# Router products of a two-layer expert stage: three bfloat16 matmuls per token from one comparison, in four PSUM banks

## What is computed

```python
def chunk(xc):
    q = (xc @ w_query).reshape(c, PEER_HEADS, 2, PEER_HALF_DIM)
    sc = jnp.einsum('chpd,hpnd->chpn', q, keys32)
    sv, si = lax.top_k(sc, PEER_TOPK)
    cand = (sv[:, :, 0, :, None] + sv[:, :, 1, None, :]).reshape(c, PEER_HEADS, -1)
    cidx = (si[:, :, 0, :, None] * PEER_N_KEYS + si[:, :, 1, None, :]).reshape(c, PEER_HEADS, -1)
    best, pos = lax.top_k(cand, PEER_TOPK)
    eidx = jnp.take_along_axis(cidx, pos, axis=-1)
    g = jax.nn.softmax(best, axis=-1)
    a = jnp.einsum('cd,chkd->chk', xc, w_up[eidx])
    act = jax.nn.gelu(a, approximate=False) * g
    return jnp.einsum('chk,chkd->cd', act, w_down[eidx])
```

## Time and profile before

| | us |
|---|---|
| median of 3 runs | 2591.95 (2590.22 to 2592.58) |
| profiled execution | 2590.26, span 2588.4 |
| TensorE busy | 2452.9 |
| VectorE busy | 1677.3 |
| ScalarE busy | 1345.7 |

### The profile page before, as it was taken

How to read it: one execution, slowest core, us unless ns; L and a number is a source line. 1 busy time by engine, 2 the same in 40 slices (tenths; PEclk the granted TensorE clock), 3 DMA queues, 4 the chain that set the end, 5 groups by cost and what they waited for, 6 DMA issues and landing times.

```text
span 2588.4 us, 44433 instructions
## 1 busy us (share of the span) xinstructions
PE 2452.9 (95%) x15412; PEld 2201.5 (85%) x15412; DVE 1677.3 (65%) x2990; ACT 1345.7 (52%) x2514; POOL 35.5 (1%) x82
## 2 busy tenths in 40 slices
PE   8989999999999998999999999999999899988988
PEld 7889999999888887989998999888888787776866
DVE  4646998777655555656998677655565537546454
ACT  4545555777555444444445777545555425534533
POOL 1000000000000000000000000000000000000000
PEclk9999999999999999999999999999999869789999
DMA  6344555444566664655555444566655523134443
GB/s 216 113 141 153 172 177 163 131 124 125 174 191 194 193 194 149 185 171 156 170 179 155 131 129 125 171 194 192 213 179 181 167 66 91 58 107 146 146 123 114
DMA packets 136853, 398.45 MB, mean 154 GB/s; under 512 B 12336, under 2 KB 13568, under 8 KB 135696
## 3 DMA queue, kind: packets, MB, share of 16 engines
q1 hardware_dynamic: 134144, 384.97, 48.3%
q0 software_dynamic: 2576, 11.71, 1.5%
HBM read 395.59 MB, written 1.05 MB: 153 GB/s over the span
## 4 chain that ended last, share of the span: by engine, by line
PE 69%; DVE 21%; ACT 5%; issue 5%; POOL 0%; DMA 0%; DVEq 0%; ACTq 0%; POOLq 0%; SPq 0%
PE bank L893 27%; PE bank L877 11%; PE bank L776 11%; PE bank L782 7%; DVE wl L1446 7%; PE bank L905 3%; ACT first L1255 2%; PE bank L843 2%; PE bank L831 2%; ACT wh L1142 1%; DVE arena L1613 1%; DVE arena L1614 1%; DVE arena L1616 1%; DVE arena L1615 1%; PE bank L974 1%
## 5 line engine op out<-in xcount | busy, mean ns | idle before, releaser
L1446 DVE TENSOR_TENSOR wl<-raw,wh 128x1024 fp32r<-128x1024 f32 (+1 forms) x732 | 893.4, 1222 | 635.0 <-ACT wh L1142 623.7
L1142 ACT ACTIVATE wh<-raw 128x1024 fp32r<-128x1024 f32 (+1 forms) x732 | 771.5, 1055 | 669.9 <-PE bank L893 341.7
L877 PE MATMUL bank<-xh,wh 128*128 128x256 f32 x2048 | 513.4, 288 | 5.3 <-issue 3.4
L877 PE MATMUL bank<-xl,wh 128*128 128x256 f32 x2048 | 502.5, 283 | 0.0
L877 PEld LDWEIGHTS bank<-xh,wh 128*128 128x128 f32 x2048 | 392.6, 192 | 7.4 <-DVE pairs L1684 3.8
L877 PEld LDWEIGHTS bank<-xl,wh 128*128 128x128 f32 x2048 | 393.2, 192 | 0.0
L877 PE MATMUL bank<-xh,wl 128*128 128x256 f32 x2048 | 293.0, 286 | 6.8 <-DVE wl L1446 6.8
L893 PE MATMUL bank<-wh,gl 128*128 128x512 f32 x1024 | 274.2, 390 | 1.7 <-DVE gl L1723 1.7
L893 PE MATMUL bank<-wh,gh 128*128 128x512 f32 x1024 | 274.0, 389 | 0.5 <-ACT gh L1272 0.5
L877 PEld LDWEIGHTS bank<-xh,wl 128*128 128x128 f32 x2048 | 262.9, 191 | 13.0 <-DVE wl L1446 11.5
L893 PE MATMUL bank<-wl,gh 128*128 128x512 f32 x1024 | 273.7, 389 | 0.0
(11 more groups left out here) (247 smaller groups left out, 2800.4 us busy)
## 6 DMA issues: line engine op xcount, KB each, us to landing
raw<-in_w_upT SPq DMA_DIRECT2D x256, 512.0 KB, 3.5
raw<-in_w_down SPq DMA_DIRECT2D x256, 512.0 KB, 3.5
raw<-in_l_w_in SPq DMA_DIRECT2D x84, 512.0 KB, 3.7
raw<-in_peer_w_query SPq DMA_DIRECT2D x32, 512.0 KB, 3.9
raw<-in_l_w_out SPq DMA_DIRECT2D x28, 512.0 KB, 3.7
raw<-in_attn_w_qkv SPq DMA_DIRECT2D x24, 512.0 KB, 4.3
raw<-in_conv_w_in SPq DMA_DIRECT2D x24, 512.0 KB, 3.8
arena<-in_na_bias POOLq DMA_DIRECT2D x4, 1024.0 KB, 6.0
```

The lines of the kernel that those rows point to most:

```text
L877: last = pe.matmul(banks[b][:, 0:SEQ], lhsT=w[part][:, k, :], rhs=x_in[xp][:, k, :], start=(k == 0 and part == 0 and xp == 0), stop=(k == ...
L1142: act.activation(wh[:, n % SPLIT, 0:kts * cols], raw[:, n % RAW, 0:kts * cols], ACT.Copy)\
L1446: tt(wl[:, n % SPLIT, 0:kts * cols], raw[:, n % RAW, 0:kts * cols], wh[:, n % SPLIT, 0:kts * cols].bitcast(F32), ALU.subtract).then_inc(lo ...
```

## The change

RING stays four; two more constants are FIRSTS = 3 (buffers of weighted first keys) and OUTS = 4 (banks for products, 2 to 5). Both one-hot rows come from one bf16 comparison against `key_pairs`. The weight is split in three bf16 parts ahead of the stage; ScalarE multiplies the first one-hot with the first part as before, VectorE with the two others. TensorE accumulates three bf16 matmuls per token with the same stationary one-hot. `idxT` takes its banks from the ring of banks 4 to 7, TensorE no longer waits for its reads, and the low parts of tiles 70 and 71 move behind the copies of each token tile. VectorE no longer waits for first_weighted; it waits for its own comparison ahead of the multiplications, and TensorE and both multiplying engines wait for the semaphores shown.

```diff
--- before.py
+++ after.py
@@ -84,7 +84,7 @@
 HALF = N_KEYS // 2
 QUAD = 4
 QUADS = SEQ // QUAD
-RING = 4
+RING, FIRSTS, OUTS = 4, 3, 4
 FIRST, SLOTS = 72, 54
 WIDE, NARROW = 4, 4
 CANDS = WIDE * TOPK + (TOPK - WIDE) * NARROW
@@ -281,16 +281,16 @@
         at = place_of["aux"]
         lanes = place("lanes", [P, N_KEYS], BF16, at)
         at += 2 * N_KEYS
-        choice = place("choice", [P, 3, SEQ], F32, at)
-        at += 4 * 3 * SEQ
-        pairs = place("pairs", [P, SEQ, 2], BF16, at)
-        at += 2 * 2 * SEQ
-        second = place("second", [P, RING, QUAD, N_KEYS], F32, at)
-        at += 4 * RING * QUAD * N_KEYS
-        chosen = place("chosen", [P, 2, QUAD, N_KEYS], BF16, at)
-        at += 2 * 2 * QUAD * N_KEYS
-        first = place("first", [P, RING, QUAD, N_KEYS], F32, at)
-        at += 4 * RING * QUAD * N_KEYS
+        weight_high = place("weight_high", [P, SEQ], F32, at)
+        at += 4 * SEQ
+        key_pairs = place("key_pairs", [P, SEQ, 2, 2], BF16, at)
+        at += 2 * 4 * SEQ
+        rest_pairs = place("rest_pairs", [P, 2, SEQ, 2], BF16, at)
+        at += 2 * 4 * SEQ
+        onehot = place("onehot", [P, RING, QUAD, 2, N_KEYS], BF16, at)
+        at += 2 * RING * QUAD * 2 * N_KEYS
+        first = place("first", [P, FIRSTS, 3, QUAD, N_KEYS], BF16, at)
+        at += 2 * FIRSTS * 3 * QUAD * N_KEYS
         late = place("late", [P, 2, SEQ], F32, at)
         at += 4 * 2 * SEQ
         gh, gl = (place(n, [P, SPLIT, SEQ], F32R, at + k * 4 * SPLIT * SEQ) for k, n in enumerate(("gh", "gl")))
@@ -369,9 +369,9 @@
                 J.add("wo", 4, own=False, ring="projection")
             J.add("na", len(na_steps(n)), ring="other")
             J.add("na_oT", NA_JOINED.count(n), ring="other")
-        J.add("norm_peer0", 4); J.add("query0", 8, own=False); J.add("scores0", 8); J.add("idxT0", 2)
+        J.add("norm_peer0", 4); J.add("query0", 8, own=False); J.add("scores0", 8); J.add("idxT0", 2, ring="other")
         J.add("norm_conv", 4); J.add("conv_in", 12, own=False); J.add("conv_out", 4, own=False)
-        J.add("norm_peer1", 4); J.add("query1", 8, own=False); J.add("scores1", 8); J.add("idxT1", 2)
+        J.add("norm_peer1", 4); J.add("query1", 8, own=False); J.add("scores1", 8); J.add("idxT1", 2, ring="other")
         J.add("norm_mem", 4, ring="projection"); J.add("mem0", 2, own=False, ring="projection"); J.add("mem1", 2, own=False, ring="projection")
         EV, OM = attention_order(sum(n for _, n in SEC)), attention_order(MEM_HEADS)
 
@@ -443,6 +443,7 @@
         top_ready, top_exp = sem("top_ready"), sem("top_exp")
         top_split = sem("choices_split")
         onehots, first_weighted = sem("onehots_ready"), sem("first_keys_weighted")
+        rests_weighted = sem("first_keys_weighted_by_rests")
         products, weighted = sem("router_products"), sem("experts_weighted")
         held, late_weighted = sem("router_weights_held"), sem("late_experts_weighted")
         gelu_done = sem("gelu_done")
@@ -897,14 +898,15 @@
 
                 def router(q):
 
-                    pe.wait_ge(onehots, q0 + q + 1)
                     pe.wait_ge(first_weighted, q0 + q + 1)
-                    if q >= 2:
-                        pe.wait_ge(weighted, q0 + q - 1)
+                    pe.wait_ge(rests_weighted, q0 + q + 1)
+                    if q >= OUTS:
+                        pe.wait_ge(weighted, q0 + q - OUTS + 1)
                     for c in range(QUAD):
-                        last = pe.matmul(banks[2 + q % 2][:, c * N_KEYS:(c + 1) * N_KEYS],
-                                         lhsT=second[:, q % RING, c, :], rhs=first[:, q % RING, c, :],
-                                         start=True, stop=True)
+                        for p in range(3):
+                            last = pe.matmul(banks[2 + q % OUTS][:, c * N_KEYS:(c + 1) * N_KEYS],
+                                             lhsT=onehot[:, q % RING, c, 1, :], rhs=first[:, q % FIRSTS, p, c, :],
+                                             start=(p == 0), stop=(p == 2))
                     last.then_inc(products, 1)
 
 
@@ -923,8 +925,6 @@
                     for i in range(3):
                         last = pe.transpose(bank(j)[:, i * P:(i + 1) * P], top_out(t, i), ident[:])
                     done(last, j)
-                for t in range(TT):
-                    wait_read(pe, J.of(f"idxT{layer}", t))
                 for t in range(FIRST - 2, FIRST):
                     up(t)
 
@@ -1248,12 +1248,12 @@
                 def weigh_first(q):
 
                     act.wait_ge(onehots, q0 + q + 1)
-                    if q >= RING:
-                        act.wait_ge(products, q0 + q - RING + 1)
+                    if q >= FIRSTS:
+                        act.wait_ge(products, q0 + q - FIRSTS + 1)
                     for c in range(QUAD):
                         c0 = q * QUAD + c
-                        ins = act.activation(first[:, q % RING, c, :], chosen[:, q % 2, c, :], ACT.Copy,
-                                             scale=choice[:, 2, c0:c0 + 1])
+                        ins = act.activation(first[:, q % FIRSTS, 0, c, :], onehot[:, q % RING, c, 0, :], ACT.Copy,
+                                             scale=weight_high[:, c0:c0 + 1])
                     ins.then_inc(first_weighted, 1)
 
                 def hold(q):
@@ -1261,7 +1261,7 @@
                     n = tiles_before(q)
                     act.wait_ge(products, q0 + q + 1)
                     act.activation(acts[:, n:N_KEYS, q * QUAD:(q + 1) * QUAD],
-                                   banks[2 + q % 2].rearrange("p (c i) -> p i c", c=QUAD)[:, n:N_KEYS, :], ACT.Copy)\
+                                   banks[2 + q % OUTS].rearrange("p (c i) -> p i c", c=QUAD)[:, n:N_KEYS, :], ACT.Copy)\
                         .then_inc(held, 1)
 
                 def gated_high(t, i=0):
@@ -1605,7 +1605,10 @@
                 part_f = scratch(5, HK)
                 pick = view(P_KEYS, PEER_HEADS, TOPK, TOPK)
                 red = scratch(PEER_HEADS)
-                assert off[0] <= ARENA
+                choice = scratch(3, P)
+                rest_of = scratch(P)
+                assert off[0] + P // 2 <= ARENA
+                rounded = place(f"rounded{layer}", [P, P], BF16, place_of["arena"] + 4 * off[0])
 
                 def top16(values, index, src, tmp):
 
@@ -1680,8 +1683,16 @@
                     j = J.of(f"idxT{layer}", t)
                     wait_filled(dve, j)
                     cols = slice(t * P, (t + 1) * P)
-                    step(dve.tensor_copy(choice[:, :, cols], bank(j)[:, 0:3 * P].rearrange("p (a b) -> p a b", a=3)))
-                    read_out(dve.tensor_copy(pairs[:, cols, :], choice[:, 0, cols].unsqueeze(2).to_broadcast([P, P, 2])), j)
+                    step(dve.tensor_copy(choice, bank(j)[:, 0:3 * P].rearrange("p (a b) -> p a b", a=3)))
+                    step(dve.tensor_copy(rounded[:], choice[:, 2]))
+                    read_out(dve.tensor_copy(key_pairs[:, cols].rearrange("p c a b -> p a c b"),
+                                             choice[:, 0:2].unsqueeze(3).to_broadcast([P, 2, P, 2])), j)
+                    dve.tensor_copy(weight_high[:, cols], rounded[:])
+                    step(tt(rest_of, choice[:, 2], rounded[:], ALU.subtract))
+                    step(dve.tensor_copy(rest_pairs[:, 0, cols], rest_of.unsqueeze(2).to_broadcast([P, P, 2])))
+                    step(tt(rest_of, rest_of, rest_pairs[:, 0, cols, 0], ALU.subtract))
+                    dve.tensor_copy(rest_pairs[:, 1, cols], rest_of.unsqueeze(2).to_broadcast([P, P, 2]))
+                    low(u0 + FIRST - 2 + t)
                 dve.wait_ge(extra_loaded["lanes"], 16 * (layer + 1))
                 q0 = QUADS * layer
 
@@ -1690,15 +1701,19 @@
                     s = q % RING
                     if q >= RING:
                         dve.wait_ge(products, q0 + q - RING + 1)
-                    if q >= 2:
-                        dve.wait_ge(first_weighted, q0 + q - 1)
-                    c0 = q * QUAD
-                    lane = lanes[:].rearrange("p (n b) -> p n b", b=2).unsqueeze(1).to_broadcast([P, QUAD, N_KEYS // 2, 2])
-                    key = pairs[:, c0:c0 + QUAD, :].unsqueeze(2).to_broadcast([P, QUAD, N_KEYS // 2, 2])
-                    tt(chosen[:, q % 2].rearrange("p c (n b) -> p c n b", b=2), lane, key, ALU.is_equal)
-                    last = tt(second[:, s], lanes[:].unsqueeze(1).to_broadcast([P, QUAD, N_KEYS]),
-                              choice[:, 1, c0:c0 + QUAD].unsqueeze(2).to_broadcast([P, QUAD, N_KEYS]), ALU.is_equal)
-                    last.then_inc(onehots, 1)
+                    c0, w = q * QUAD, N_KEYS // 2
+                    hot = onehot[:, s].rearrange("p c a (n b) -> p (c a) n b", b=2)
+                    lane = lanes[:].rearrange("p (n b) -> p n b", b=2).unsqueeze(1).to_broadcast([P, 2 * QUAD, w, 2])
```

(17 more changed lines are left out.)

## The result

The median of six runs is 2547.87 us (2537.03 to 2551.42), against 2591.13 us (2589.76 to 2592.58) for the kernel before: a ratio of 0.9826 with a 95% interval of 0.9804 to 0.9847, 43.3 us less. The profiled execution took 2551.42 us (span 2549.5), 38.9 us less in the span. Of eleven further runs of the kernel before, taken beside r1 to r4, one took 3329.7 us at a mean granted clock of 0.669 and counts in no comparison; the median of the other ten is 2591.56 us.

The account below looks back on a forecast made before the run. TensorE was taken to set the pace, VectorE having some 60 us to spare. Per layer -9.3 - 11.3 + 1.9 + 1.0 = -17.7 us, two layers -35.4, gave 2556.5 us, range 2548 to 2584.

Parts of the forecast that it names:

- The waits for banks: Late expert tiles: four product banks remove 8.9 us of TensorE waits and 2.4 of cold starts, 11.3 us per layer.
- The cover that I named for ScalarE in double places: Where two quads fall between the same two tiles: 0.85 us before ScalarE's lateness makes TensorE wait; failing is an 8% rival.
- The router's matmuls: Router, 64 quads per layer: twelve bf16 pairs at 0.062 us take 0.744 us instead of 0.89, gaining 9.3 us per layer.
- The slow pairs: Rival at the router: a bf16 pair takes 0.111 us like an fp32 record, +19 us per layer, 2630 us; 8%.
- the half-hidden load: Rival at the router: half the weight load shows, 0.080 us a pair, only -4.9 us per layer, 2582 us; 9%.
- VectorE at its limit: Late expert tiles: VectorE, at 1.40 us per quad, just keeps up; TensorE's waits for low parts cost 1.0 us per layer.
- the cost of the last tile, 3.74 us: End of the stage: VectorE's work per tile, with its quads, set against TensorE's 3.76 us, so nothing to spare.
- my own ends: VectorE's work per tile with its quads: 3.31 us early in the stage, 3.74 us at its end.
- the rival with quicker pairs: Router: pairs of 0.055 us, VectorE holding the last third, bring 4 us more per layer, about 2549 us; 10%.
- Ahead of the stage: From the transposes to the first tiles: VectorE's longer work before each low part costs 1.9 us per layer, 1 to 3.
- the clock at 1.5 us either way: Behind the transposes in layer 1: whether the clock falls to 1.2 GHz again was left open, 1.5 us either way.

Follow-up runs that it names:

- r1: The changed kernel run again with nothing altered: 2543.07 us median, ratio 0.9825 to the kernel before.
- r4: The changed kernel with only VectorE's order ahead of the stage altered, low parts of weight tiles before the copies: 2537.27 us median, ratio 0.9798 to the kernel before.
- r2: The kernel before with four product banks instead of two and nothing else: 2561.16 us median, ratio 0.9882.
- r5: The changed kernel without the third matmul per token, executed once: 194.2 us from router(0) to the first down tile, against 204.6.
- r3: The changed kernel with two product banks instead of four: 2571.11 us median, ratio 0.9918 to the kernel before.
- r7: The changed kernel with three product banks instead of four, executed once: 204.6 us from router(0) to the first down tile, as with four.

## Why the prediction was right in its direction and short in its size

Of the 43.3 us, the two stages and their passages carry 20.2 + 21.5 = 41.7 us in the profile (238.0 to 217.8 us, and 239.4 to 217.9 us, from the transposes to down). The forecast had 35.4. The difference of 6.3 us has three terms; the rest of the program gives 1.6 us in the medians, and the median of before itself came out 0.8 us lower with more runs (2591.13 for 2591.95). That makes up the 8.6 us.

*The waits for banks: right.* 11.3 us per layer, by r2 to the tenth. This is more than half of what the change brings, and needs none of its bf16 work. The cover that I named for ScalarE in double places held: no wait for scalings or a high part in the stage.

*The router's matmuls: mechanism right, term too small. This is the largest error.* I took 0.062 us a pair from small fp32 pairs; it takes 0.056 us, within 3 ns of 128 cycles of 2.4 GHz. What I put at nothing is the way from the tile to the pairs and back, 0.07 us in each of 54 places. Per layer 54 quads became 0.16 us cheaper and ten 0.23 us, which gives the measured 10.9 us (r2 to the changed kernel) where I had 9.3. That is 3.2 us of the error in both layers. The two mistakes work against each other: the cheaper pairs bring 64 x (0.23 - 0.146) = 5.4 us more per layer than I had, and the places take back 54 x 0.07 = 3.8. So that 9.3 came as near as it did is in part luck. My own 0.057 us (cycles plus the 4 ns of the same line) was the better price of a pair, but it would have given 13.2 us, further off. The slow pairs (0.111 us) and the half-hidden load (0.080 us) are excluded: the loads of 128 bf16 columns add at most 3 ns to the spacing. With them falls the sentence of the Trainium skill (TensorE: Matmul & The Clock Gate, "Back-to-back issue gap") on a stream of pairs at about 81 ns: here it is 56 ns, near what the same page's isolated gap gives.

*VectorE at its limit: wrong.* I charged 1.0 us per layer, 2.0 in all; measured is none. The durations were right (1.40 us per build, to the hundredth). The step that failed compared the cost of the last tile, 3.74 us, with TensorE's 3.76 and made waits of it. That the last tiles have nothing to spare was right (VectorE is busy for 99% of the time from 620 to 640 us), but TensorE did not wait. Up to there VectorE needs less than TensorE and gets ahead, so the sum over the stage counts: the mean of my own ends, 3.53 us over 54 places, is 190 us, and r5 measured a floor of 194.2 at most against 204.6. The same step held up the low end of the range: I let VectorE stop the rival with quicker pairs at 2549 us. By its sum it would have stopped nothing before 194 us per stretch, and without it that rival comes to about 2544 us (5.4 us per layer off the forecast, and the 1.0 us gone).

*Ahead of the stage: right in layer 0, too dear in layer 1.* I said 1.9 us per layer; it is 2.0 and 0.7. The steps came as listed, and the low parts behind the copies are what costs, as r4 shows. In layer 1 the kernel before had already lost 1.3 to 1.4 us to a low clock (12.6 us against 11.2 in its layer 0 and 11.3 in r2 at full clock). The changed kernel takes 13.3 us there whether its clock falls or not, so it has 1.3 us less to lose. I had put the clock at 1.5 us either way; the error in the sum is 1.1 us.

*The rest of the program.* By the medians it is 1.6 us shorter (2591.13 - 2547.87 = 43.3, less 41.7), in the first profile 2.8 us longer, in that of r1 6.0 us shorter, in that of r4 10.1 us shorter. I did not foresee this spread: the three runs of before that I had lay within 3 us. Why the kernel before stays put while r1 to r4 and the changed kernel vary by 7 to 14 us was not found out; no run here separates the clock's own timing from the program's. With a median that can move by some us for this reason, a range whose low end was 8 us below its centre was too narrow on that side.

## What to carry to other kernels

Before new arithmetic is built to shorten an engine's work, look in the chain for the place where it waits for a buffer: here one constant, the wait that goes with it and three indices gave 11.3 us per layer, and the three-part products 8.9 more (10.9 in the stage, less 2.0 ahead of it). Three banks did as much as four. Whether a second engine will bind was decided here by its sum over the stage, not by its dearest step; leave part of the bounding engine's work out to measure the distance. Whatever stands in a queue ahead of work that the bounding engine waits for is a cost at a stage's start, even where the stage itself has room, and a change of order may take it back.

## What the runs showed of the hardware

A pair of load and matmul with 128 bf16 columns, the same weights loaded three times, runs at 0.056 us at the 2.4 GHz level (a second quad of twelve in 0.67 us). The fp32 records of 128 columns run at 0.111 us. Going from the matmuls of a tile to the bf16 pairs and back costs 0.07 us more than going to the fp32 pairs, so short groups of cheap matmuls between others gain less than their own spacing says. A VectorE comparison of 1024 bf16 elements takes 0.68 us; two multiplications back to back start 0.34 us apart, and a wait on the engine's own last instruction lets the next start 0.04 us after its end, where without a wait it starts 0.08 us before it (0.34 us from start to start at a duration of 0.42).

Around the six transposes the granted clock of one and the same program fell to the 1.2 GHz level in some executions and not in others. TensorE's longest wait there is 1.7 us in the kernel before and 1.8 us in the changed one. In the kernel before the clock fell in layer 1 and not in layer 0, in r2 in neither. In the changed kernel it fell in both layers of the first profile, in r1 in layer 1 alone, and in r3 and r7, whose code is the same up to router(0), in neither layer and in layer 0 alone. The same program, in code untouched by any change, has been granted mean clocks from 0.964 to 0.971, and the times go with it over 16 us (2552.8 to 2537.0).
